# Expert mixer: gates in 8 groups of four chunks, one part of the gates kept on chip, value tables loaded first and four deep

## The reference

```python
def peer_ffn(h, w_query, sub_keys, u_tab, v_tab):
    q = (h @ w_query).reshape(B, L, PEER_HEADS, 2, PEER_QDIM // 2)
    s = jnp.einsum('blhtd,htnd->blhtn', q, sub_keys).astype(F32)
    s1, i1 = lax.top_k(s[..., 0, :], PEER_TOPK)
    s2, i2 = lax.top_k(s[..., 1, :], PEER_TOPK)
    ...
    top, pos = lax.top_k(cand, PEER_TOPK)
    idx = jnp.take_along_axis(cidx, pos, axis=-1)
    g = jax.nn.softmax(top, axis=-1).astype(h.dtype)
    ...
        act = jax.nn.gelu(jnp.einsum('td,tkd->tk', hx, u_tab[ix]))
        return jnp.einsum('tk,tkd->td', gx * act, v_tab[ix])
```

## Time and profile before

| | us |
|---|---|
| median of 3 runs | 2948.17 |
| profiled execution | 2943.05 |
| its span | 2941.2 |
| TensorE busy | 2554.2 (87%) |
| VectorE busy | 2377.8 (81%) |
| ScalarE busy | 1197.0 (41%) |
| GpSimd busy | 644.6 (22%) |

### The profile page before, as it was taken

How to read it: one execution, slowest core, us unless ns; L and a number is a source line. 1 busy time by engine, 2 the same in 40 slices (tenths; PEclk the granted TensorE clock), 3 DMA queues, 4 the chain that set the end, 5 groups by cost and what they waited for, 6 DMA issues and landing times. The chain is left out here.

```text
span 2941.2 us, 44148 instructions
## 1 busy us (share of the span) xinstructions
PE 2554.2 (87%) x16181; PEld 2260.1 (77%) x16181; DVE 2377.8 (81%) x4626; ACT 1197.0 (41%) x1806; POOL 644.6 (22%) x486
## 2 busy tenths in 40 slices
PE   7976897789999999997888888887779999999765
PEld 3964797789999999995667778786668888888553
DVE  7877679977999999999962655589968788888877
ACT  3344343763333333332343224444644444444332
POOL 0000053001111112223200000251324334343552
PEclk9987899999999999999988998898989999999988
DMA  5720333579998989989941313244889999999985
GB/s 216 276 70 26 144 128 121 190 277 321 305 314 298 314 308 308 313 293 293 304 148 66 114 57 130 86 138 164 317 327 351 336 352 354 355 340 345 333 309 192
DMA packets 333353, 708.38 MB, mean 241 GB/s; under 512 B 172848, under 2 KB 175696, under 8 KB 326368
## 3 DMA queue, kind: packets, MB, share of 16 engines
q1 hardware_dynamic: 272896, 466.60, 46.9%
q0 software_dynamic: 55360, 201.38, 18.5%
q10 hardware_dynamic: 4896, 37.75, 3.2%
HBM read 640.89 MB, written 64.72 MB: 240 GB/s over the span
## 5 line engine op out<-in xcount | busy, mean ns | idle before, releaser
L1996 PE MATMUL pe_s<-hl_hi,pq_uh 128*128 128x320 f32 (+2 forms) x2304 | 718.2, 312 | 48.9 <-DVE pq_ul L163 25.1
L1997 PE MATMUL pe_s<-hl_lo,pq_uh 128*128 128x320 f32 (+2 forms) x2304 | 706.9, 307 | 0.0
L1998 PE MATMUL pe_s<-hl_hi,pq_ul 128*128 128x320 f32 (+2 forms) x2304 | 705.3, 306 | 0.0
L2079 PE MATMUL peer_acc<-val_vh,val_w 128*128 128x512 f32 x2048 | 613.8, 403 | 85.6 <-DVE val_w L163 85.3
L2079 PEld LDWEIGHTS peer_acc<-val_vh,val_w 128*128 128x128 f32 x2048 | 386.2, 193 | 181.2 <-DVE val_vl L163 103.3
L1996 PEld LDWEIGHTS pe_s<-hl_hi,pq_uh 128*128 128x128 f32 x2304 | 450.8, 196 | 72.0 <-issue 38.4
L1997 PEld LDWEIGHTS pe_s<-hl_lo,pq_uh 128*128 128x128 f32 x2304 | 451.0, 196 | 8.5
L1998 PEld LDWEIGHTS pe_s<-hl_hi,pq_ul 128*128 128x128 f32 x2304 | 450.2, 195 | 0.0
L2253 POOL DMA_INDIRECT pe_frow<-in_peer_rows,pe_fidx x192 | 234.1, 1219 | 876.1 <-DVE pe_frow L2413 813.3
L2253 POOL DMA_INDIRECT pe_frow<-in_peer_v,pe_fidx x192 | 286.0, 1489 | 496.8 <-DVE pe_fh L2429 232.5
L2197 ACT ACTIVATE val_vh<-val_vr 128x1024 fp32r<-128x1024 f32 x256 | 270.6, 1057 | 259.3 <-DMA val_vr<-in_peer_v 229.0
(11 more groups left out here) (489 smaller groups left out, 3990.0 us busy)
## 6 DMA issues: line engine op xcount, KB each, us to landing
pq_ur<-in_peer_u SPq DMA_DIRECT2D x256, 512.0 KB, 4.5
val_vr<-in_peer_v SPq DMA_DIRECT2D x256, 512.0 KB, 5.7
gates<-gate_stg ACTq DMA_DIRECT2D x30, 1024.0 KB, 7.3
val_mrow<-in_ada_rows SPq DMA_DIRECT2D x56, 512.0 KB, 7.4
val_gr<-gates SPq DMA_DIRECT2D x128, 160.0 KB, 5.8
pq_ur<-in_w_query SPq DMA_DIRECT2D x32, 512.0 KB, 3.5
s_wv<-val_out SPq DMA_DIRECT2D x32, 512.0 KB, 7.9
val_gr<-gates SPq DMA_DIRECT2D x128, 128.0 KB, 7.1
```

The costliest lines, as they stand in the source:

```text
L1996: pe.matmul(o, r32(uh[:, b, k]), r32(hi[:, k, a:T]), start=k == 0, stop=False)
L1997: pe.matmul(o, r32(uh[:, b, k]), r32(lo[:, k, a:T]), start=False, stop=False)
L1998: mm = pe.matmul(o, r32(ul[:, b, k]), r32(hi[:, k, a:T]), start=False, stop=k == KC - 1)
L2079: mm = pe.matmul(acc[:, 2 * t + c, :], r32(lhs[:, b, w]), r32(rhs[:, b, c * 512:(c + 1) * 512]), start=False, stop=False, skip_group_check ...
```

## The change

In layer 1 the gate stage has 8 groups of four chunks in place of 16 of two. `LAST` becomes 26 and `RING` 30. The last part of the gates (part 3) is held: it isn't stored, and `apply` multiplies its 64 columns directly by the half of `stg` that keeps it. The other three parts are read back for four blocks at a time, 384 KB in one DMA. There are four value buffers, two of them where the one-hot tiles were, and a value table is loaded four blocks ahead. The ring of fetched rows has seven places. In both layers the value table's load stands ahead of the score table's load in a slot. The counts of layer 0 stay as they were. The arithmetic is unchanged.

The diff, with most unchanged lines left out:

```diff
...
-    def __init__(self, fetched, groups, early):
+    def __init__(self, fetched, groups, held, each, values, early):
+        self.held, self.each, self.values = held, each, values
+        self.stored = self.parts - held
+        self.odd_stored = (self.parts + 1) // 2 - held
...
-PLANS = Plan(64, [3] * 12 + [2] * 2, 0), Plan(128, [2] * 16, 32)
+PLANS = Plan(64, [3] * 12 + [2] * 2, 0, 1, 2, 0), Plan(128, [4] * 8, 1, 4, 4, 32)
...
-RING_ROWS = 3, 5
+RING_ROWS = 3, 7
...
-    FROM, TOKENS = plan.first, plan.tokens
+    FROM, TOKENS, EACH, VALUES = plan.first, plan.tokens, plan.each, plan.values
+    held = plan.stored * HALF
...
-        gr = x.sb("gr", [P, 2, PARTS, HALF])
+        gr = x.sb("gr", [P, 2, plan.stored, EACH * HALF])
         if layer == 0:
-            x.sb("kept", [P, 2 * NKEYS * HALF - 6 * D - 2 * TOKENS])
+            x.sb("kept", [P, 2 * NKEYS * HALF - 6 * D - 2 * plan.stored * EACH * HALF])
+        spare_vr = x.sb("more_vr", [P, VALUES - 2, D]) if VALUES > 2 else None
+    def loaded_value(n):
+        return vr[:, n % VALUES] if n % VALUES < 2 else spare_vr[:, n % VALUES - 2]
     if layer == 0:
...
-    uload, vload, gload = ([s.sem(f"{k}{b}_loaded") for b in range(2)] for k in "uvg")
+    uload, gload = ([s.sem(f"{k}{b}_loaded") for b in range(2)] for k in "ug")
+    vload = [s.sem(f"v{b}_loaded") for b in range(VALUES)]
...
-            def value(n, b):
+            def value(n):
-                sp.dma_start(vr[:, b], src.rearrange("a p m -> p (a m)")).then_inc(vload[b], 16)
-            def gate(n, b):
-                src = gates_dram[0:PARTS, :, bass.ds(n, 1), :]
-                sp.dma_start(gr[:, b], src.rearrange("h p a c -> p h (a c)")).then_inc(gload[b], 16)
+                sp.dma_start(loaded_value(n), src.rearrange("a p m -> p (a m)")).then_inc(vload[n % VALUES], 16)
+            def gate(m):
+                src = gates_dram[0:plan.stored, :, m * EACH:(m + 1) * EACH, :]
+                sp.dma_start(gr[:, m % 2], src.rearrange("h p a c -> p h (a c)")).then_inc(gload[m % 2], 16)
...
             for n in range(LOW + 2, RING + 2):
-                    value(0, 0)
-                    value(1, 1)
+                    value(0)
+                    value(1)
-                    sp.wait_ge(gst1, 16 * ((PARTS + 1) // 2))
-                    gate(0, 0)
-                    gate(1, 1)
+                    sp.wait_ge(gst1, 16 * plan.odd_stored)
+                    if plan.held:
+                        sp.wait_ge(gst2, 16 * (PIECES - 1) * plan.odd_stored)
+                    gate(0)
+                    gate(1)
+            for n in range(2, VALUES):
+                value(n)
             def slot(z):
+                if z.has(VALUES):
+                    sp.wait_ge(vlow, z.n + 3)
+                    value(z.n + VALUES)
                 if z.has(RING + 2):
                 if z.has(2):
-                    sp.wait_ge(vlow, z.n + 3)
-                    value(z.n + 2, b)
-                    sp.wait_ge(applied, z.n + 1)
-                    if z.n + 2 >= SOON:
-                        sp.wait_ge(gst2, 16 * ((PIECES - 1) * ((PARTS + 1) // 2 - 1) + 2))
-                    gate(z.n + 2, b)
+                    if (z.n + 1) % EACH == 0 and z.n + 1 + EACH < NB:
+                        sp.wait_ge(applied, z.n + 1)
+                        if z.n + 2 >= SOON and not plan.held:
+                            sp.wait_ge(gst2, 16 * ((PIECES - 1) * (plan.odd_stored - 1) + 2))
+                        gate((z.n + 1) // EACH + 1)
                 if layer == 0:
...
-                if c >= full:
+                if full <= c < plan.stored * (full + 1) + full:
             def store_piece(c, part, k):
...
             def value_high(z, ahead):
-                act.wait_ge(vload[b], z.turn(ahead) * 16 + 16)
+                n = z.n + ahead
+                act.wait_ge(vload[n % VALUES], n // VALUES * 16 + 16)
-                nc.scalar.activation(r32(vh[:, b]), vr[:, b], copy).then_inc(vhigh, 1)
+                nc.scalar.activation(r32(vh[:, b]), loaded_value(n), copy).then_inc(vhigh, 1)
             def gated_high(z, ahead):
...
-            act.wait_ge(evacd, CHUNKS)
-            store_rest(PARTS - 1, SOON, SOON + REST)
+            if not plan.held:
+                act.wait_ge(evacd, CHUNKS)
+                store_rest(PARTS - 1, SOON, SOON + REST)
             def slot(z):
...
                 if z.has(RING + 1):
-                if z.n == 0:
+                if z.n == 0 and not plan.held:
             for n in range(NB):
...
             def apply(z, ahead):
-                b = (z.n + ahead) % 2
-                dve.wait_ge(gload[b], z.turn(ahead) * 16 + 16)
-                dve.wait_ge(drained, z.n + (ahead + J + 3))
-                a = A[:, z.place(ahead)]
-                v.tensor_tensor(a, a, gr[:, b].rearrange("p h c -> p (h c)"), ALU.mult).then_inc(applied, 1)
+                n = z.n + ahead
+                m, at = n // EACH, n % EACH * HALF
+                dve.wait_ge(gload[m % 2], m // 2 * 16 + 16)
+                dve.wait_ge(drained, n + (J + 3))
+                a = A[:, z.place(ahead), 0:held].rearrange("p (h c) -> p h c", c=HALF)
+                ins = v.tensor_tensor(a, a, gr[:, m % 2, :, at:at + HALF], ALU.mult)
+                if plan.held:
+                    a = A[:, z.place(ahead), held:TOKENS]
+                    ins = v.tensor_tensor(a, a, stg[:, 1, n], ALU.mult)
+                ins.then_inc(applied, 1)
             def value_low(z, ahead):
-                lo_part(nc, vl[:, b], vr[:, b], vh[:, b]).then_inc(vlow, 1)
+                lo_part(nc, vl[:, b], loaded_value(z.n + ahead), vh[:, b]).then_inc(vlow, 1)
             def gated_low(z, ahead):
```

## The result

The changed kernel takes 2870.02 us, the median of 4 runs (2867.64 to 2871.87), against 2948.35 for the kernel before on the same chip: a ratio of 0.973, 95% interval 0.9708 to 0.9752. The profiled execution has a span of 2865.8 us for 2941.2, 75.4 less.

The account below looks back on a forecast made before the run. Layer 1's gate stage was taken as bound by VectorE, its steady loop by transfers over a TensorE floor of 5.61 us. Gate stage -9.1, filling -10.9, loop and tail -29.1 gave -49.1: 2899 us against the median, range 2876 to 2938.

Parts of the forecast that it names:

- the two DMA waits: Layer 1's steady loop: ScalarE's 94.0 us for value tables and VectorE's 81.4 us for gates would go.
- Steady loop: Layer 1 slots with score and value products: 5.75 us each, between 5.61 and the old 6.05; 96 slots, 552.0 us.
- Tail: Layer 1 slots with value products alone: 4.45 us each, between 4.09 and 4.81; 29 intervals, 129.1 us.
- Filling: Pipeline start behind layer 1's gate stage: the interval before block 2 shrinks to a slot, -10.9 us, bounds 0 and -16.
- The gate stage itself: Layer 1, bound by VectorE: 8 `table_low` fewer, -9.1 us, bounds 0 and -10.
- the split `apply`: Layer 1's `apply` as two instructions: 0.06 us extra on VectorE, bounds 0 and 0.17.
- the landing of the score table: Layer 1's steady loop: lands 6.7 us after issue behind a value table, no stall, 1.9 us to spare.
- layer 0 at nothing: Layer 0 gets only the new load order, hidden by TensorE work: 0 us, bounds -3 and +5.
- The demand worked out for the engines: Layer 1's steady loop: DMA demand per slot falls from 5.87 to about 5.5 us, just under TensorE's 5.61.
- Floors reached: Rival: steady slots of 5.61 and tail slots of 4.15 us, -76 us, 2872 in all; chance 0.05.
- Bytes are the bound: Rival: the byte rate, 345 GB/s, limits layer 1's loop, so fewer packets gain nothing; -20 us, 2928; chance 0.22.
- Late score tables: Rival: with two score-table buffers, landings past 9.8 us slow layer 1's loop; +18 us, 2966; chance 0.07.

Follow-up runs that it names:

- e5: The changed kernel with layer 1's value loads as before: two buffers, queued behind the score table's load; 2921.1 us.
- e9: The changed kernel with six of the fetched rows moved from the tail to the steady loop; 2866.6 us.
- e2: The changed kernel with two value buffers in layer 1 instead of four, the value load still ahead of the score table's; 2889.6 us.
- e8: The changed kernel with gates read one block at a time (256 B pieces, 96 KB), part 3 still held; 2902.8 us.
- e10: The kernel before with only the change's value loads: ahead of the score table's load, four buffers; 2925.2 us.
- e6: The changed kernel with part 3 of the gates stored and read back like the other parts, four blocks a read; 2878.9 us.
- e1: The changed kernel with each four-block gate read split into four DMAs of 96 KB in 256 B pieces; 2875.6 us.

## Why the prediction was wrong

The way was right and the size was not: the two DMA waits went as forecast, but the steady loop and the tail together gave 53.9 us for 29.1, because both were priced between the floor and the old time.

**Steady loop: 5.75 taken, 5.62 measured, 12.7 us.** I had the floor of 5.61 and moved off it because the DMA engines "would be at 0.96 or more". That step failed. It took the 0.44 us that a slot lost before for engine time, and the share of 0.97 for its proof. e5 has the 0.44 at a share of 0.93; the changed kernel and e9 have none at 0.98 and 0.99. The trace before already had what decides. A value buffer is free when `value_low` has ended; its next load stood behind `table_low` on the sync queue, as here:

```profile
2403.07 1.22 DVE L163 TENSOR_TENSOR val_vl<-val_vr,val_vh 128x1024 fp32r<-128x1024 f32 x1
...
2406.20 0.61 SPq L1916 DMA_DIRECT2D val_vr<-in_peer_v  x1
```

That is 1.9 us, and 1.9 at the median. The 390.4 us of rows 6 are no measure of it: they count how long the queue stood there, mostly before the buffer was free, and in the changed kernel it stands 419.1 us in 88 slots (312.4 and 106.7) while TensorE loses nothing. I named the late issue and then priced the engines' time.

**Tail: 4.45 taken, 4.03 measured, 12.2 us.** My floor was 4.09. I took the middle between it and 4.81 because some products had run at 1.2 GHz. The clock was low where TensorE waited: with e2's waits it stands at 0.96, without them at 1.00, and at 1.00 a slot's products (some 2.9 us) don't hold VectorE up. So I carried over as a loss of its own what went with the waits. What the slow products themselves added to the old 4.81 no run separates. What the tail needed was depth in the value loads (e2, 4.50) and gates asked for ahead (e8, 4.55); with both it is at VectorE's time.

**Filling: -10.9 forecast, -15.2 measured**, inside my bound of -16. Both causes that I gave act, the stores that are gone (e8 against e10) and the reading ahead (e6 against e10), and either nearly suffices. The interval before block 2 shrank from 16.6 to 5.8 us, as priced; the other 4.4 us are block 1, which came that much sooner and which I had only in the bound.

**What held.** The gate stage itself (-8.9 for -9.1), VectorE's 0.06 us for the split `apply`, the landing of the score table (6.8 for 6.7), layer 0 at nothing. The demand worked out for the engines, 5.5 us a slot, agrees with 0.98 x 5.62 = 5.5, but e8 and e1 have the same pieces at shares that give 5.70 and 5.65, so a share times a slot is a demand only to some 0.1 us.

**The rivals.** "Floors reached" was the outcome (2872 for 2870), and I gave it 0.05. That its sum fits to 2 us is in part luck: its loop is 2.6 us too long, its filling 0.8 too short, and 3.4 us were lost behind block 127. "Bytes are the bound" is refuted: 345 GB/s was not a limit, the loop ran at 370. The Trainium skill ("DMA: Bandwidth & Descriptors", Specifications) has some 358 GB/s of HBM per core, as half of what a stack gives its two cores; for this kernel on one core it is no ceiling, 370 GB/s being held for 540 us. The same table wants 512 B at least for line rate; e1's 288 pieces of 256 B more in a slot cost 0.03 us of the slot and took the share from 0.98 to 1.00, so the trace shows them cheap here, not free. "Late score tables" didn't come: 7.3 us of waits, landing 6.8, far under the 9.8 from which it would decide. They are the next in line: in e6, with 512 KB reads of gates, ScalarE waits 23.9 us for them between 2210 and 2660 us.

## What to carry to other kernels

Before pricing a transfer by bytes and pieces, write down its buffer's round: from the last reader's end to the issue (what stands before it on the issuing queue), the landing, and the copies; divided by the number of buffers it must stay below the slot. In these traces a DMA share near 1 proved neither that the engines bind nor that they don't; undo the lateness first. Where two waits lie side by side, mending one shows little (18.7 and 4.9 us here, 62.0 together), so ask of each fix what the other wait would then do, and if all are mended, forecast the floor of the next engine and not a mean with the old time.

## What the runs showed of the hardware

- One core moved 370 GB/s over the 540 us of the steady loop, 374 in e9, at shares of 0.98 and 0.99; before, 0.97 went with 345 GB/s. The share moved by 0.01 to 0.02 while the rate rose by 7 and 8%. It is no measure of the room that is left.
- The granted clock was low where TensorE waited: 0.89 in the tail before, 0.96 in e2's, 1.00 after, with the same products in each slot.
- Beside two stores of 1.5 MB in flight, loads landed late: a 128 KB read of gates took 16.9 us in e10, and ScalarE waited 13.4 us for a score table in e6. The same reads of gates in the steady loop landed in 7.6 us (before).
